# One head's weights scaled ahead of the last rotations, and expert rows gathered one expert sooner

## What is computed

```python
def attn_projections(h, w_in, g_qa, g_ka):
    p = h @ w_in                      # qa, ka, va, qb, kb, vb
    qa = rms_norm(heads(qa), g_qa)    # group A only
    ka = rms_norm(heads(ka), g_ka)
# latent q and k of both groups are rotated (rope_2d)
# group A: 8 heads, full attention over 512 latent + 128 context keys
# group B: 8 heads, window of 128 tokens + 128 context keys, learned sink logit
def one_block(q_blk):
    s = einsum(q_blk, k) * scale
    p = softmax(s)                    # group B: softmax_with_sink
    return einsum(p, v)
x = x + gt1 * rms_norm(concat(oa, ob) @ w_out, g_post_attn)

def expert_choice_moe(h, w_router, w_gate, w_up, w_down):
    aff = softmax(h @ w_router)       # 16 experts
    g, idx = top_k(aff.T, 2 * T // 16)    # each expert takes 64 latent, 16 context rows
    xg = h[idx]
    y = (silu(xg @ w_gate) * (xg @ w_up)) @ w_down * g
    return zeros.at[idx].add(y)
```

## Time and profile before

| | |
|---|---|
| median of 3 runs | 942.31 us (941.33 to 944.38) |
| the profiled execution's own time | 943.21 us |
| its span, first to last instruction | 941.2 us |
| PE busy | 886.7 us (94%) |
| DVE busy | 365.0 us (39%) |
| ACT busy | 216.1 us (23%) |
| POOL busy | 101.8 us (11%) |
| mean granted clock of PE | 0.988 of full |

### The profile page before, as it was taken

One profiled execution on the slowest core, in us unless ns is written; L12 is line 12 of the kernel. 1 busy time (PEld: TensorE's weight loads), 2 busy tenths in 40 slices (PEclk: granted clock), 3 DMA queues, 4 the chain that ended last, 5 costly groups with the idle time before them and its releaser, 6 DMA issues. The chain is left out here.

```text
span 941.2 us, 19933 instructions
## 1 busy us (share of the span) xinstructions
PE 886.7 (94%) x8653; PEld 442.4 (47%) x8653; DVE 365.0 (39%) x974; ACT 216.1 (23%) x528; POOL 101.8 (11%) x137
## 2 busy tenths in 40 slices
PE   3999998899899999899999999999999999999984
PEld 3544444777656665643444444344344343433431
DVE  4255635887767765811112031111113120310136
ACT  3132223666644653410000000000000000000012
POOL 1021200000000000100111011011101100110225
PEclk9999999999999999989999999999999999999997
DMA  9997532600001119679999999999999999999983
GB/s 341 350 367 282 202 156 82 226 2 1 2 1 46 45 53 373 246 258 410 398 397 408 397 398 395 411 398 397 407 400 398 396 410 397 398 401 384 350 308 153
DMA packets 77717, 269.31 MB, mean 286 GB/s; under 512 B 6208, under 2 KB 9984, under 8 KB 77632
## 3 DMA queue, kind: packets, MB, share of 16 engines
q1 hardware_dynamic: 72384, 251.42, 68.5%
q0 software_dynamic: 4160, 13.90, 5.1%
q10 hardware_dynamic: 1088, 2.74, 0.7%
HBM read 252.06 MB, written 15.99 MB: 285 GB/s over the span
## 5 line engine op out<-in xcount | busy, mean ns | idle before, releaser
L962 PE MATMUL ps<-ring,reg 128*32 128x512 f32 x1792 | 201.6, 592 | 0.0
L1824 DVE TENSOR_SCALAR mod<-ps,kt 64x512 f32<-64x512 f32 x30 | 22.5, 750 | 255.9 <-PE ps L962 255.7
L962 PEld LDWEIGHTS ps<-ring,reg 128*32 128x32 f32 x1792 | 58.1, 110 | 112.8 <-issue 104.2
L976 PE MATMUL ps<-ring,values_in 128*32 128x256 f32 x1536 | 93.6, 385 | 2.3 <-ACT reg L1331 1.1
L1335 ACT ACTIVATE reg<-ps 128x256 f32<-128x256 f32 x16 | 6.1, 383 | 366.0 <-PE ps L1016 354.8
L962 PE MATMUL ps<-ring,kt 128*32 128x512 f32 x768 | 86.8, 592 | 0.0
L818 PE MATMUL ps<-ring,reg 128*128 128x512 f32 x160 | 76.4, 604 | 0.0
L976 PEld LDWEIGHTS ps<-ring,values_in 128*32 128x32 f32 x1536 | 49.6, 111 | 52.5 <-issue 22.0
L664 PE MATMUL ps<-ring,reg_qt 128*128 128x512 f32 x160 | 70.6, 594 | 0.0
L976 PE MATMUL ps<-ring,reg 128*32 128x256 f32 x1024 | 61.9, 384 | 2.5 <-DMA ring<-in_w_down 2.0
L1278 ACT ACTIVATE ring<-ps 128x640 f32<-128x640 f32 (+3 forms) x80 | 44.3, 554 | 72.2 <-PE ps L747 69.6
(11 more groups left out here) (238 smaller groups left out, 1003.2 us busy)
## 6 DMA issues: line engine op xcount, KB each, us to landing
ring<-in_w_up SPq DMA_DIRECT2D x32, 2048.0 KB, 22.5
ring<-in_w_down SPq DMA_DIRECT2D x32, 2048.0 KB, 22.6
reg_qt<-in_w_gate SPq DMA_DIRECT2D x16, 2048.0 KB
ring<-in_w_gate SPq DMA_DIRECT2D x16, 2048.0 KB
ring<-in_w_ada SPq DMA_DIRECT2D x12, 2048.0 KB, 12.2
reg<-in_x_sample SPq DMA_DIRECT2D x8, 512.0 KB, 6.4
ring<-in_w_in SPq DMA_DIRECT2D x2, 2048.0 KB, 17.0
ring<-in_w_out SPq DMA_DIRECT2D x2, 2048.0 KB, 10.0
```

What stands on the lines that cost most here:

```text
L962: last = pe.matmul(o[64 * n + r:64 * n + r + 32, :], x(4 * hf + j, r), w[:, j, n * HALF:(n + 1) * HALF], start=(hf == 0 and j == 0), stop= ...
L976: last = pe.matmul(o[32 * q:32 * q + 32, :], x(c), w[:, j, q * QUART:(q + 1) * QUART], start=(c == 0), stop=(c == KC - 1))
L1824: dve.tensor_scalar(put_l[:, n * HALF:(n + 1) * HALF], ps[rows, 3, :], g_l[rows, e:e + 1], None, ALU.mult)
```

## The change

Five edits, none of which adds or removes an instruction:

1. DVE scales unit 0 (a new function `normalise(0)`, the same two instructions) right after `low_part(13)`, ahead of `maxima(1)` and `low_part(14)`. `low_part(14)` follows `maxima(1)`.
2. `rbias` and `rotate_last` move from before `maxima(1)` and after unit 0 to behind unit 1's scaling.
3. `nsink` moves to behind unit 6's scaling.
4. `turn_qk(15)` on PE moves from the loop at u = 1 to u = 3, behind `values(0)`; `high_part(15)` on ACT from u = 2 to u = 3, behind `exponentials(4)`. `low_part(15)` on DVE keeps its place behind unit 3's scaling.
5. POOL gathers the rows of pairs 2 to 7 one expert sooner; pairs 0 and 1 as before.

```diff
@@ PE, loop over units
-                if u == 1:
+                if u == 3:
                     turn_qk(3 * TILES)
@@ ACT, loop over units
-                if u == 2:
+                if u == 3:
                     high_part(3 * TILES)
@@ DVE, before the loop over units
             low_part(3 * TILES - 2)
-            dve.wait_ge(consts_in, 16 * N_CONSTS)
-            link(dve.tensor_scalar(nsink[:, :], sink[:, :], -1.0, None, ALU.mult))
-
-            low_part(3 * TILES - 1)
+
+            def normalise(u):
...
+                dve.wait_ge(exp_done, u + 1)
...
+                link(dve.reciprocal(rden[:, b:b + 1], den[:, b:b + 1]))
+                dve.tensor_scalar(probs[:, u % 3, 0:n], probs[:, u % 3, 0:n], rden[:, b:b + 1], None, ALU.mult)\
+                    .then_inc(probs_ready, 1)
+
+            normalise(0)
...
-            dve.wait_ge(shift_spread, 1)
-            dve.tensor_copy(rbias[:, :], ps[:, 7, 0:2 * E]).then_inc(router_set, 1)
@@ DVE, loop over units
+                if u:
+                    normalise(u)
                 if u == 0:
+                    low_part(3 * TILES - 1)
+                if u == 1:
+                    dve.wait_ge(shift_spread, 1)
+                    dve.tensor_copy(rbias[:, :], ps[:, 7, 0:2 * E]).then_inc(router_set, 1)
                     rotate_last()
                 if u == 3:
                     low_part(3 * TILES)
+                if u == 6:
+                    dve.wait_ge(consts_in, 16 * N_CONSTS)
+                    link(dve.tensor_scalar(nsink[:, :], sink[:, :], -1.0, None, ALU.mult))
@@ POOL, loop over experts
-                if e % 2 == 0 and e + 2 < E:
-                    pool.wait_ge(xe_turned, e + 2)
-                    gather_l(e // 2 + 1)
+                if e == 0 or e % 2 and e + 3 < E:
+                    pair = (e + 1) // 2
+                    pool.wait_ge(xe_turned, 2 * pair + 2)
+                    gather_l(pair + 1)
```

More of the change, by code:

```diff
@@ L1592, in _ @@
             low_part(3 * TILES - 2)
-            dve.wait_ge(consts_in, 16 * N_CONSTS)
-            link(dve.tensor_scalar(nsink[:, :], sink[:, :], -1.0, None, ALU.mult))
-            low_part(3 * TILES - 1)
+            def normalise(u):
+                g, h, t = HEAD_UNITS[u]
+                n, b = key_count(g, t), u % 2
+                dve.wait_ge(exp_done, u + 1)
+                if g:
+                    n_sink[0] += 1
+                    dve.wait_ge(sink_exp, n_sink[0])
+                    link(dve.tensor_tensor(den[:, b:b + 1], den[:, b:b + 1], esink[:, b:b + 1], ALU.add))
+                link(dve.reciprocal(rden[:, b:b + 1], den[:, b:b + 1]))
+                dve.tensor_scalar(probs[:, u % 3, 0:n], probs[:, u % 3, 0:n], rden[:, b:b + 1], None, ALU.mult)\
+                    .then_inc(probs_ready, 1)
+            normalise(0)
             def rotate_last():
```

## The result

| | before | after |
|---|---|---|
| median | 941.95 us (6 runs, 941.33 to 944.38) | 949.24 us (6 runs, 945.87 to 951.09) |
| ratio | | 1.0074, 95% interval 1.0062 to 1.0086 |
| profiled execution, its own time | 943.21 us | 945.87 us |
| its span | 941.2 us | 943.8 us |
| mean granted clock | 0.988 | 0.987 |

The change is slower, 7.3 us by the medians. I had forecast 3.6 with an upper end of 947.5 us, so the sign was right and the size was not. The six times spread over 5.2 us, where those of before spread over 3.1, and the execution that was profiled is the shortest of the six. The spread is part of the answer.

What follows compares the result with a forecast made beforehand. DVE bounds the start of attention, PE 180 to 350 us, PE and DMA the experts. +2.3 (late low part) +1.3 (clock) +0 (gathers) = +3.6 on 942.31 gives 945.9 us; 8 in 10 range 942.6 to 947.5.

Steps and rivals of the forecast that it cites:

- DVE's walk: Start of attention: DVE's queue is full without gaps; unit 0 is ready 2.7 us sooner, which pays only if DVE ends sooner.
- The rival of the other side: PE's 3.84 us idle before unit 0 really bounds: -2.7 to -3.9 us, time 938.4 to 939.6; chance 0.06.
- The new wait: Before `low_part(15)`: DVE idles 2.6 us for the late turned tile, unit 5 is turned 2.3 us later; +2.3 us.
- The rival that the stall is hidden: DVE's wait before `low_part(15)` is hidden or doesn't arise: 942.3 us, or 942.1 with unit 0 sooner; chance 0.12.
- 172.7 and 1.3: PE before unit 4: last tile turned by 172.7, then unit 3 and scores(6), 1.3 us behind `turn_qk`.
- The clock: PE's wait of about 3.2 us before unit 4 brings a likely half-clock spell over the work behind it: +1.3 us.
- It may begin or end inside them, so I take 1.3: Half-clock spell over turning unit 4, scores(7) and `values(1)`: 1.7 us if over all, taken as 1.3.
- my upper end for it (3.2): The clock's upper end, 3.2 us, with a second half-clock spell around PE's 2.4 us wait for unit 2.
- the 1.7 that I had for the whole steps: Half clock over all of turning unit 4, scores(7) and `values(1)`: 0.42, 0.42 and 0.85, together 1.7 us.
- The gathers: Experts: PE's 0.6 us wait for gathered rows goes but returns as waits for w_down; 0, between -0.6 and 0.
- Slower by over 0.3%: Whole kernel slower by more than a measurement can tell from no change, 0.3% or 2.8 us; chance 0.56.
- the case with two full spells: Start of attention: late low part plus two half-clock spells, up to 2.3 + 3.2 = +5.5 us, 947.8 us.

Runs made afterwards that it cites:

- before_held: Before, with 30 dummy matmuls in PE's 3.84 us wait for unit 0: 943.2 us median of 12, ratio 1.0009.
- turn_at_two: The changed kernel with the last tile's `turn_qk` and `high_part` at u = 2 instead of u = 3: 942.59 us median of 12, ratio 0.9996.
- held_less: The changed kernel with 6, 4, 8 and 9 dummy matmuls in PE's waits before units 0, 1, 2 and 4: 944.84 us median of 12, ratio 1.0025.
- turn_late: Before, with only the last tile's `turn_qk` and `high_part` moved to u = 3: 949.0 us median of 6, ratio 1.0065.
- again_2: The changed kernel without edit, a single execution for another trace: 952.63 us.
- again_3: The changed kernel without edit, one more single execution for a trace: 950.56 us.
- second series: The changed kernel timed once more without edit: 950.12 us median of 7 (945.01 to 952.21), ratio 1.0065.
- again: The changed kernel once more without edit, for a second trace and more times: profiled execution 948.04 us, median of 7 950.12 us, ratio 1.0065.
- attention: The changed kernel with its gathers put back as before: 948.15 us median of 7, ratio 1.0063.

## Why the prediction was right and wrong

**DVE's walk, right.** The stretch is bound by DVE, unit 0 came 2.6 us sooner (PE turned it at 161.91, and at 164.54 before) and nothing was gained by it. before_held delayed unit 0 by 2.7 us at a price of 0.6, and turn_at_two kept the early unit 0 and came out level. The rival of the other side, that PE's first idle counts, falls by both.

**The new wait, right.** "DVE stands idle for 2.6 us" and "+2.3 us": held_less measured 2.53 us, and 2.3 us in the median. turn_late shows that this one edit makes the loss, turn_at_two that undoing it ends it. The rival that the stall is hidden falls. Two waits of PE were read wrong on the way. The one before unit 2 was to be 2.4 us and was 1.28 in after, where the work ahead of it ran at half clock; and scores(3) waited 1.20 us for unit 1's exponentials, a wait that the prediction doesn't have. The end of PE's work before unit 4 should also have been 174.0 by the prediction's own terms (172.7 and 1.3), not 173.8. None of these moves the +2.3.

**The clock, the failed step.** It is "It may begin or end inside them, so I take 1.3". The mechanism was right, the size was not: the whole change is 7.3 us over before by the first medians and held_less 2.3, so the clock costs some 5 us, and my upper end for it (3.2) was below that. Two things were left out of the sum. First, I priced the long wait before unit 4 and put the spell around the shorter waits into the bound only. In all five traces of the whole attention part the clock fell there already, between 162.4 and 164.8 us, and stayed down for 10.2 us in four of them and 13.7 us in again_2, although in after PE was busy 7.57 of the 10.2 us. The chain scores(5), `values(0)`, turned tile is just what DVE's wait hangs on, so the spell went straight into it: DVE waited 4.89 us in after for 2.53 in held_less. That is 2.4 us, the largest single piece. Second, where the clock falls again behind the wait before unit 4, it takes all of unit 4, scores(7), `values(1)` and part of unit 5: 180.44 to 185.10 in again_2, 4.66 us, for 179.73 to 182.25 in after, 2.52. That is 2.1 us, near the 1.7 that I had for the whole steps. From held_less to again_2 the distance grows by 5.3 us in all. I had both spells together only as the upper end; again_3, an execution near the second series' median (950.56 for 950.12), has both in full.

The rows of before could have told more. The half-clock prices 1.29 and 1.41 us were at hand. Put into the walk for unit 2, scores(5) and `values(0)` they make the tile 1.7 us later, and its own transposes at 1.05 make it 0.4 more. I put them into the sum for one place only.

The Trainium skill's rule (TensorE: Matmul & The Clock Gate, "HAM oscillation"), that only an idle gap above some length bites, would have given +2.3. Here the clock fell after waits of 1.2 us with work between them, in again_2 within 0.1 us behind the first of them (1.19 us), so these traces disagree with it as a rule on single gaps; I was right to go by the rows and didn't go far enough.

**The gathers, right.** Put at 0, measured at 0.9996 (0.9985 to 1.0007), with PE's wait moved from rows to weights, 0.6 us for 0.6. By the rule of the Trainium skill, DMA: Bandwidth & Descriptors ("Rules for kernel authors"), to issue early and wait late, the 0.6 us would have been saved. The wait itself did go, as the rule says, and the time did not.

**The chances.** "Slower by over 0.3%" had 0.56 and came true. The range was too narrow above, because the case with two full spells was cut off as the unlikely tail.

## What to carry to other kernels

Before moving work so that a visible wait shrinks, ask whether the engine waited for is full there: if it is, its own order is free to choose, and what counts is when the things arrive that it waits for itself. When a producer's step moves behind others, follow it through every queue to the consumer, and ask what stands behind the consumer's waiting instruction. And price that chain once at full clock and once at half, since splitting one long wait of PE into several short ones can take the clock down along the very chain that became critical.

## What the runs showed that I had not expected

- One wait of 3.84 us in before costs nothing and its half-clock spell costs nothing. In after, waits of 1.20, 1.20, 1.35 and 1.28 us, with work between them, come with 10.2 us of half clock, in which PE was busy for 7.57.
- A spell of half clock in the same place is there in one execution and absent in the next: behind the wait before unit 4 `values(1)` took 1.31 us in after (clock 0.99 over 174.8 to 182.2) and 2.40 in again, again_2, again_3 and attention. The times of the changed kernel spread over 7.2 us in the second series, in part for this reason, and two or three executions would have told little of the size.
- With the clock at full from 17 to 925 us the kernel was no faster than before (1.0002), and PE's waits for w_down rose by 1.6 us.
